# Forget attention and norms of prompt tiles 1 to 3 in the expert stage, the samples' state rule among the delta levels

## What is computed

```
def token_mixers(h, ...):                       # h = adaLN(RMSNorm(x); c)
    proj = h @ w_in                             # one projection, split into gq gk gv gz ga gb fq fk fv ff
    q, k, v = silu(causal_conv(gq, gk, gv));  q, k = l2norm(q) * HEAD_DIM**-0.5, l2norm(k)
    o, S = gated_delta_chunked(q, k, v, g, beta, s0)      # 8 heads x 64, a triangular solve per chunk
    o = rms(o) * gdn_norm_w * silu(gz)
    # forgetting attention (FoX), 8 heads x 64
    s = q @ k.T * HEAD_DIM**-0.5 + Fq - Fk;  o_fox = softmax(where(k_pos <= q_pos, s, -inf)) @ v
    return concat(o, o_fox) @ w_out             # samples: k, v, F go on from 2048 cached rows in 16 pages each

x = x + g1 * token_mixers(...)
x = x + g2 * peer(adaLN(RMSNorm(x); c))         # 8 heads, each picks 16 of 16384 experts by two sets of 128 keys
    act = gelu(pu[eidx] @ x) * gate;  out = act @ pv[eidx]
```

## Time and profile before

| | us |
|---|---|
| median of 3 runs | 2018.28 |
| the 3 runs | 2019.94, 2012.95, 2018.28 |
| profiled execution | 2011.07 |
| its span, first to last instruction | 2009.2 |
| PE, DVE, ACT, POOL busy in it | 1467.6, 1332.7, 660.8, 799.1 |
| DMA: bytes, mean rate | 726.93 MB, 362 GB/s |

### The profile page before, as it was taken

One profiled execution on the slowest core, in us unless ns is written; L12 is line 12 of the kernel. 1 busy time (PEld: TensorE's weight loads), 2 busy tenths in 40 slices (PEclk: granted clock), 3 DMA queues, 4 the chain that ended last, 5 costly groups with the idle time before them and its releaser, 6 DMA issues. The chain is left out here.

```text
span 2009.2 us, 30900 instructions
## 1 busy us (share of the span) xinstructions
PE 1467.6 (73%) x10644; PEld 824.2 (41%) x10644; DVE 1332.7 (66%) x3076; ACT 660.8 (33%) x1990; POOL 799.1 (40%) x581
## 2 busy tenths in 40 slices
PE   6999988877877985666698666668866666676434
PEld 4445456565655552442365244335523441121001
DVE  4346666654478876656887566688768568776754
ACT  2111132121134442324454232344533233432322
POOL 0277751203015543335444333444524345344441
PEclk9998999988988997789698777869977896556555
DMA  7487758956679999999999999999999999999996
GB/s 310 131 301 234 246 181 271 334 196 215 225 309 385 420 420 421 423 421 421 413 421 421 422 421 420 420 399 422 419 414 418 422 420 395 418 415 421 421 422 264
DMA packets 130919, 726.93 MB, mean 362 GB/s; under 512 B 17120, under 2 KB 19041, under 8 KB 58437
## 3 DMA queue, kind: packets, MB, share of 16 engines
q0 software_dynamic: 75024, 545.82, 65.7%
q1 hardware_dynamic: 55741, 179.15, 24.5%
HBM read 715.92 MB, written 9.09 MB: 361 GB/s over the span
## 5 line engine op out<-in xcount | busy, mean ns | idle before, releaser
L2657 POOL DMA_INDIRECT RING<-in_peer_uv,R x390 | 454.7, 1166 | 666.3 <-PE bank L510 533.5
L2392 DVE SCALAR_TENSOR_TENSOR RING<-RING,MV 128x1024 f32<-128x1024 f32 x384 | 469.3, 1224 | 288.8 <-DMA RING<-in_peer_uv,R 264.4
L510 PE MATMUL bank<-RING,R 128*32 128x512 f32 (+1 forms) x1560 | 293.3, 806 | 293.8 <-ACT R L1460 273.0
L510 PE MATMUL bank<-R 128*128 128x128 f32 (+5 forms) x2184 | 346.6, 425 | 128.4 <-ACT R L1460 115.7
L510 PEld LDWEIGHTS bank<-R 128*128 128x128 f32 (+4 forms) x2184 | 240.7, 189 | 260.2 <-issue 247.9
L1470 ACT ACTIVATE R<-R 128x2 f32<-128x2 f32 x256 | 52.0, 203 | 774.2 <-DVE RING L2392 649.6
L2657 POOL DMA_INDIRECT R<-in_peer_uv,R x130 | 151.8, 1168 | 205.4 <-PE bank L510 184.6
L510 PE MATMUL bank<-R,ident 128*32 128x4 f32 (+5 forms) x2500 | 200.8, 276 | 10.8 <-ACT R L1432 2.6
L2392 DVE SCALAR_TENSOR_TENSOR R<-R,MV 128x1024 f32<-128x1024 f32 x128 | 156.5, 1223 | 77.1 <-DMA R<-in_peer_uv,R 61.4
L510 PEld LDWEIGHTS bank<-RING,R 128*32 128x32 f32 (+1 forms) x1560 | 41.1, 122 | 400.7 <-issue 393.1
L510 PEld LDWEIGHTS bank<-HT,R 128*128 128x128 f32 x992 | 137.0, 220 | 55.5 <-issue 55.5
(11 more groups left out here) (336 smaller groups left out, 1742.5 us busy)
## 6 DMA issues: line engine op xcount, KB each, us to landing
R<-in_peer_wq SPq DMA_DIRECT2D x12, 2048.0 KB
RING<-in_w_mod SPq DMA_DIRECT2D x11, 2048.0 KB, 9.0
R<-in_cache_v SPq DMA_DIRECT2D x84, 256.0 KB, 3.6
MV<-in_cache_k SPq DMA_DIRECT2D x64, 256.0 KB, 3.9
R<-in_cache_k SPq DMA_DIRECT2D x64, 256.0 KB, 3.5
R<-in_w_out SPq DMA_DIRECT2D x6, 2048.0 KB
MV<-in_cache_v SPq DMA_DIRECT2D x44, 256.0 KB, 3.9
RING<-in_peer_uv,R POOLq DMA_INDIRECT x390
```

Of the source, the lines that this page charges most:

```text
L510: i = nc.tensor.matmul(out, lhsT, rhs, start=start, stop=stop, **k)
L2392: V.scalar_tensor_tensor(u, u, 1.0, QUARTER[s_ % 4], ALU.mult, ALU.mult, accum_out=DOT[:, n % 4, s_:s_ + 1]).then_inc(S("dots"), 1)
L2657: nc.gpsimd.indirect_dma_start(UV[g % UN], None, a["peer_uv"][0], bass.IndirectOffsetOnAxis(ap=idx, axis=0)).then_inc(S(f"uv_in{g % UN}"), 16)
```

## The change

- The FoX loop shrinks to 12 steps and the 8 units of tile 0. `late_scores`, `late_turn`, `late_values` and `fox_exp`, `fox_max`, `fox_turned`, `fox_norm` with a tile number do tiles 1 to 3 in the expert stage, from events 12, 120 and 248 on (`fox_slots`), with the norms of that tile behind them. The rest of the tile's slots moves on and is packed closer: two halves of a query part and two of an output part stand at one event.
- What the late tiles need is stored in the first stage: keys (`fk_d`), queries twice (`fq_d`, for even and odd heads), forget rows (`forget_d`). Before each tile's FoX SP loads five pieces of it (`foxin`), the values from `out_v_prompt`. The tokens of tiles 1 to 3 are stored before their norms.
- Value groups 0 to 3 are used in the loop, then four in each of the seven levels. Three of the modulation chunks are in the loop, five at the end of levels 0 to 4. The sample state lies in ring slot 1, so chunks 12 to 19 all use slot 0, each loaded only when the one before has been used; the last, 20, waits until the state rule is done with slot 1.
- The state rule's steps stand in levels 0, 1, 3, 4, 5 and behind the last level, POOL's products behind the masks of levels 3, 5 and 6; its gate stands behind the norm of tile 0, and the samples' turned output at event 3.

```diff
--- before.py
+++ after.py
-            return (0, 1 if m < 48 else 3, 2)[m % 3]
+            return (0, 2, 7)[(m - 32) % 3]
...
-        SS0 = part(R2, 0, 4096, k=HD, v=HD)
-        SSP = part(R2, 4096, 4096, k=HD, v=HD)
-        SSPV = part(R2, 4096, 4096, v=HD, k=HD)
+        SS0 = part(RING[:, 1, :], 0, 4096, k=HD, v=HD)
+        SSP = part(R1, 10240, 4096, k=HD, v=HD)
+        SSPV = part(R1, 10240, 4096, v=HD, k=HD)
...
+        def late_fox(i):
+
+            w, n = P * (i + 1), 2 if i == 3 else 4
+            return (part(R2, 0, 4 * w, j=4, t=w), part(R2, 4 * w, (i + 1) * WID, t=i + 1, c=WID),
+                    part(R2, 5120 if i == 3 else 3072, n * w, n=n, c=w), part(R2, 6144 if i == 3 else 3072 + n * w, n * w, n=n, c=w))
+        LATE_K, LATE_V, LATE_P, LATE_PT = zip(*((None,) * 4 if i == 0 else late_fox(i) for i in range(TILES)))
+        LATE_Q = [None] + [[part(R2, (4096 if i == 3 else 6144) + x * 512, 512, j=4, c=P) for x in range(2)] for i in range(1, TILES)]
+        FOX_SLOTS = (2, 4, 4, 2)
+        LATE_FORGET, LATE_FOX = R2[:, 7168:7680], R2[:, 7680:8192]
...
-        slot_of = [n if n < 4 else n % 2 for n in range(len(chunks))]
+        slot_of = [n if n < 4 else n % 2 if n < 12 else n // 20 for n in range(len(chunks))]
...
-        FOX_STEPS = 34
-        LEVELS_END = FOX_STEPS + 7 * LATE
-        MOD_AT = (1, 4, 7, 10, 13, 16, 19, 22)
+        FOX_STEPS = 12
+        LEVELS_END = FOX_STEPS + 7
+        MOD_AT = (0, 4, 8, 12, 13, 14, 15, 16)
...
-            return 10 + n if n < 16 else FOX_STEPS + (max(0, (n - 16) // 2 - 1) if LATE == 1 else (n - 16) * 7 * LATE // 16)
+            return (9, 10, 10, 11)[n] if n < 4 else FOX_STEPS + n // 4 - 1
...
+        def fox_slots(i):
+
+            slots = []
+            for g in range(4):
+                a, b = 2 * g, 2 * g + 1
+                if i == 1:
+                    slots += [(2 * g + 5, "fv", a), (2 * g + 5, "fv", b), (2 * g + 2, "ft", a), (2 * g + 2, "ft", b), (2 * g, "fs", a), (2 * g, "fs", b)]
+                else:
+                    slots += [(4 * g + 6, "fv", a), (4 * g + 7, "fv", b), (4 * g + 3, "ft", a), (4 * g + 4, "ft", b), (4 * g, "fs", a), (4 * g + 1, "fs", b)]
+            end = (0, 14, 22, 22)[i]
+            slots += [(-2, "foxin"), (end - 1, "foT")] + [(end - 5 + x, "norm", x) for x in range(4)]
+            return end, sorted(slots, key=lambda s_: (s_[0], ("norm", "fv", "ft", "fs", "foT", "foxin").index(s_[1])))
...
-        FIRST_EVENT = {1: 10, 2: 8, 3: 8}
+        FOX_EVENT = {1: 12, 2: -8, 3: -8}
...
+            start = (tile - 1) * PH * STEPS + FOX_EVENT[tile]
+            end, fox = fox_slots(tile)
+            for at, *s_ in fox:
+                slots_at.setdefault(start + at, []).append((tile, *s_))
+            event = FOX_EVENT[tile] + end - 1
+            for s_ in delta_slots() + post_slots(tile):
+                event += not (s_[0] == "wo" and (s_[2] == TILES or s_[3] % 2) or s_[0] == "wq" and s_[3] or s_ == ("tokens", 1) or tile == 1 and s_ == ("rest", 6))
                 slots_at.setdefault((tile - 1) * PH * STEPS + event, []).append((tile,) + s_)
...
                 for lv in range(7):
                     solve(i, 0, lv)
                     solve(i, 1, lv)
-                    sample_turns(FOX_STEPS + 7 * i + lv)
-                    if lv >= 3:
-                        out_turn(lv - 3, 1)
+                    sample_turns(FOX_STEPS + lv)
+                    if lv == 3:
+                        out_turn(0, 1)
                     for hb in range(2):
                         if 0 < lv < 6:
                             correct(i, hb, lv, "X")
                         if lv:
                             correct(i, hb, lv, "Y")
+                    if FOX_STEPS + lv in MOD_AT:
...
+            def fox_exp(i, h):
+
+                n, w = 8 * i + h, P * (i + 1)
+                b = full_bank(act, ("sc", n))
+                act.wait_ge(S("fox_max"), n + 1)
+                if h >= FOX_SLOTS[i]:
+                    job_done(act, ("pT", n - FOX_SLOTS[i]))
+                A((LATE_P[i] if i else PR)[:, h % FOX_SLOTS[i], 0:w], b[:, 0:w], ACT.Exp, bias=NM[:, n:n + 1], accum_out=RS[:, n:n + 1]).then_inc(free(("sc", n)), 1)
+
+            for u in range(8):
...
+            between = {0: sample_scores, 1: sample_conv, 2: sample_max, 3: write_decays, 4: sample_shift, 5: first_squares, 6: sample_exp_sums,
+                       7: lambda: norm_sums(0), 8: sample_probs, 9: norm_first, 10: new_values}
...
-                    if i == 0:
-                        if 2 <= lv <= 4:
-                            norm_scale(lv - 1)
-                        if 1 <= lv <= 3:
-                            norm_sums(lv)
-                            settle()
-                            dve.wait_ge(S("gdn_ss"), lv + 1)
-                            dve.sem_inc(S("sq_free"), 1)
+                    if FOX_STEPS + lv in MOD_AT:
+                        mod_row(4 + MOD_AT.index(FOX_STEPS + lv), 4 + MOD_AT.index(FOX_STEPS + lv))
+                    if lv == 0:
+                        srule_norms()
+                    elif lv == 1:
+                        srule_scale()
+                    elif lv == 3:
+                        for x in range(4):
+                            srule_sums(1, x)
+                        srule_new()
+                    elif lv in (4, 5):
+                        srule_state(2 * lv - 8)
+                        srule_state(2 * lv - 7)
...
+            for x in range(4):
+                srule_sums(3, x)
+            srule_out()
...
+                    if lv in (3, 5, 6):
+                        state_product((lv - 2) // 2)
...
+            sp.wait_ge(S("fk_ready"), 4)
+            store(fk_d, FK.rearrange("p j t -> p (j t)"), "fox_out")
             chunk(11)
-            chunk(12)
+            for i in range(TILES):
+                job_read(sp, ("frow", i))
...
+                job_done(sp, last_job[11])
+                sp.wait_ge(S("spilled"), stored["spilled"])
...
+            job_read(sp, ("cvT", 10))
+            job_read(sp, ("cvT", 11))
+            for t in range(LATE, TILES):
+                store(gt_d[t], GT[:, t, :], "spilled")
+            for t in range(LATE, TILES):
+                job_read(sp, ("gz", t))
+                store(gz_d[t], GZ[t], "spilled")
+            sp.wait_ge(S("fox_zero"), 2)
+            for x, q in enumerate((FQ, FQO)):
+                store(fq_d[x], q.rearrange("p j t -> p (j t)"), "fox_out")
+            next_mod(4)
...
+            value_pages(0)
+            value_pages(1)
+            value_pages(2)
...
+            for n in range(3, 32):
+                value_pages(n)
+                if n % 4 == 2 and value_turn(n) - 1 in MOD_AT[3:]:
+                    next_mod(4 + MOD_AT.index(value_turn(n) - 1))
+            sp.wait_ge(S("srule"), 4)
+            store(o["delta_sample"][0].rearrange("b h k v -> (b h) (k v)"), SS0[0:64].rearrange("p k v -> p (k v)"), "srule_stored")
+            load(WR_ROWS[0], wq[0, :, 0:2048], "keys_in")
+            for sem in ("mod_out0", "mod_out1"):
+                sp.wait_ge(S(sem), 256)
+            load(G1, mod_d[0:1, 2 * D_MODEL:3 * D_MODEL].to_broadcast([P, D_MODEL]), "g1_in")
+            sp.wait_ge(S("srule_stored"), 16)
+            sp.wait_ge(S("srule_pool"), 3)
+            chunk(20)
...
+            late_in(LATE)
+            sp.wait_ge(S("srule"), 6)
+            store(samp_d[:, 5, :].rearrange(by_head, h=8), SV[0:64, 4, :], "srule_stored")
+            sp.wait_ge(S("srule_stored"), 32)
+            load(OGS, samp_d[:, 5, :], "ogs_in")
...
+                elif kind == "foxin":
+                    job_done(sp, ("qT", i - 1, 3, 3))
+                    n = P * (i + 1)
+                    load(LATE_K[i], fk_d.rearrange("p (j t) -> p j t", j=4)[:, :, 0:n], "fox_in")
+                    for x in range(2):
+                        load(LATE_Q[i][x], fq_d[x].rearrange("p (j t) -> p j t", j=4)[:, :, i * P:(i + 1) * P], "fox_in")
+                    load(LATE_FORGET[:, 0:n], forget_d[:, 0:n], "fox_in")
+                    load(LATE_V[i], o["v_prompt"][0, 0, 0:n].rearrange("(t p) h d -> p t (h d)", p=P), "fox_in")
```

315 lines of the change are left out of this document (147 added, 168 removed).

## The result

| us | before | changed |
|---|---|---|
| median | 2017.42 (4 runs) | 2132.26 (2130.62 to 2136.52, 4 runs) |
| span of the profiled execution | 2009.2 | 2134.7 |
| first gather | 573.1 | 601.1 |
| from the first gather to the end | 1436.1 | 1533.6 |

The ratio is 1.0575 (95% interval 1.055 to 1.060): the change makes the kernel 5.75% slower. Both stages are longer: the first by 28.0 us, where 22.5 less were forecast, the expert stage by 97.5, where 22 more were. Against the forecast the first stage is 50.5 us off and the expert stage 75.5.

The account below looks back on a forecast made before the run. The prediction took the expert stage as bound by DMA bytes, the first stage only setting the first gather. Span: 2009.2 - 22.5 (first stage) + 19 (loads) + 3 (lost transfer) = 2008.7 us; median 2018, range 2000 to 2040.

Parts of the forecast that it names:

- The expert stage is set by its bytes: Expert stage: each added MB costs 2.4 us; the late tiles' 6.88 MB of loads were taken as +19 us.
- Lost transfer in the expert stage: Expert stage: moments when PE and DVE fall short despite eight gather buffers, put at 3 us, bounds 0 and 15.
- The second rival: Start of tiles 2 and 3: engines fall behind the gather buffers, +24 instead of +3, 2039 us; chance 0.19.
- both slower rivals: Expert stage's engines falling behind (chance 0.19) and first stage not getting shorter (chance 0.08), each put at 2039 us.
- step 5: Delta levels: each of five levels, with four value groups and one modulation step, takes 20.2 us by SyncE's issues.
- The third rival: First stage: late modulation chunks lengthen five levels by 4 to 5 us, nothing is gained, 2039 us; chance 0.08.
- The loop with 34 steps is nearly as slow as its page stream: FoX loop before the change: SyncE's page groups, 4.3 us each without a wait, nearly set its pace.
- State load 10 us later: First stage: new stores and copies delay the state load from 319.29 to about 329 us.
- After the last level +1, or 6 if the cover were gone: Behind the last level: four last state-rule sums fill a DVE gap, costing +1 us, or 6 without that gap.
- What would show it: List of signs: first gather between 546 and 556 us, expert stage some 22 us longer, dips behind late FoX loads.
- The bound of 565 for the first gather: End of first stage: the prediction is wrong if the first gather comes later than 565 us.

Follow-up runs that it names:

- e4: Changed kernel with the late tiles' data stored as it lies in memory and loaded back in two or three packed loads instead of five; 2095.39 us, ratio 1.0401.
- e2: Changed kernel with each of the five loads ahead of a late tile's FoX bringing one partition's row, not 128; 2081.01 us, ratio 1.0333.
- f2: Changed kernel with two value groups used at a level's start and two behind its corrections, not all four at the start; 2104.68 us, ratio 1.0443.
- b1: Kernel before, with the value pages' numbers written into the program so that SyncE reads none; 2005.53 us, ratio 0.995.
- b2: Kernel before, with the page numbers of value groups 0 to 11 read ahead of time where SyncE stands idle; 2015.23 us, ratio 0.9999.
- f3: Changed kernel with the state rule's last four sums placed before VectorE's wait for the samples' turned values; 2124.67 us, ratio 1.0546.
- e3: Changed kernel with the late queries stored one tile after the other, so they come back in rows of 2 KB; 2126.16 us, ratio 1.0571.

## Why the prediction was wrong, point by point

- **The expert stage is set by its bytes.** Right for the kernel before, and as far as bytes go for the changed one: the bytes alone make 16.7 us at the rate of before, where 16.5 to 21.3 were given. e4 against e2, packed loads at full size against none, is 18.5 us of measured stretch, with 5 us more of waiting for loads in it; I had taken 19. (By the rule of the Trainium skill, DMA: Bandwidth & Descriptors, Specifications, that pieces from 512 B up go at line rate, it would be 16.5; the runs agree nearly for the sum, 16.7 to 18.5, and the rule does not give the time until a load is there, 39 us.) The step that failed is the one after it.
- **Lost transfer in the expert stage: 3 us, bounds 0 and 15.** 80.8 us were measured, nearly all of it in two parts: 39 from how the loads are cut up (e4), 39.8 from the engines (e2). The averages (970 and 926 of 1360 us) said that there was room, and the earlier trace rows that eight buffers cover a stall. But in that stall the DMA share stayed at 1.01, so it was shorter than the buffers last; the three new ones were not. The second rival named the right place, what "is waited for by PE before its first FoX score", and priced it at 24 us with a chance of 0.19. Its 8 us a tile are near what 2.9 MB take at 417 GB/s (7.0 us), and not the 39. The price of short pieces was taken as a rate (303 against 417 GB/s), which was fine for the bytes' sum; as a delay beside the gathers it was missed. Even with both slower rivals at once the working gave some 2061 us. No row of the kernel before that I had read shows this delay, and I gave it no bound.
- **A level takes 20.2 us (step 5).** It took 24.6 to 27.0, and this step holds 30 of the 50.5 us by which the first stage was off. I added up SyncE's issues and did not lay them against what releases them. The order shows both facts: all four groups stand at a level's start, and the fourth is behind the row of the level before. The third rival had nearly the right size (4 to 5 us a level) from another cause, a chunk that comes late: in the trace TensorE does not wait for the chunk (446.42) but for the fourth group. I refuted it with "chunk and row are needed 17 us apart, the chain needs 15.5", which left out that group. f2 repairs exactly this and gives 28.4 us.
- **"The loop with 34 steps is nearly as slow as its page stream."** As a cause wrong for the most part. Without any reading the loop is 7.4 of 132.6 us shorter (b1), with a third of the groups read ahead not at all (b2), where the groups went out 4.4 to 4.7 us apart, released by TensorE. A queue that is never seen waiting may be just as fast as what it feeds.
- **State load 10 us later.** 333.0 where about 329 was forecast; group 3 and the first page product of level 0 within 5 us of the working (381.3 against 376).
- **After the last level +1, or 6 if the cover were gone.** It was gone: from the projection's start to the turned output 15.9 us against 9.0. f3 gave 3 of them back. The second half of the projection took 2.5 us more at the lower clock, which I had not priced.
- **What would show it.** The bound of 565 for the first gather caught the first stage, and the dips behind the FoX loads that were to speak for the second rival are there; for the expert stage I had given no upper bound.

## What to carry to other kernels

A load that must land before an in-order engine goes on is not priced by its bytes alone when other traffic runs beside it; how it is cut into pieces counts too (39 us against 9 to 18 here). Store data in the layout in which it will be read back, in runs of several KB, before thinking of hiding it. When work is moved into a stage that lives from buffered transfers, what counts is not the average room of the engines but the fullest stretch behind it and, as I read the dips, how many buffers are full when it begins. And a cycle's length is the sum of one queue's issues only if nothing else holds them up (f2, 20.2 us, against 24.6 to 27.0): write down for each issue what releases it, and look for the step that waits for the end of the cycle before.

## What the runs showed of the hardware

- A plain load issue can hold SyncE for 10.7 to 12.0 us (the forget rows of tiles 1 and 2, behind 1536 pieces of keys and queries on the way). The same instruction takes 4.2 us at tile 3, behind as many pieces, 0.4 us with 768 pieces ahead of it (e3), and packed loads take 0.3 to 0.5 us each (e4).
- The DMA engines' share is no measure of rate: 0.98 with 376 GB/s (1040 to 1080 us) and 1.01 with 421 GB/s (1100 to 1200 us) stand in the same kernel, e2.
- 2.3 MB in 2048 pieces took 39 to 49.5 us beside gathers until TensorE had them; packed into two loads they landed after 11.4 and 15.3 us (e4).
- TensorE's granted clock in the last 60 us ahead of the first gather was 0.97 in the kernel before (near its level of 2.4 GHz), where TensorE had been busy for 42 of the 53 us ahead of them, and 0.83 in the changed one, where it had been busy for 86 of 135; the same 16 products took 7.1 and 9.6 us.
